# The state-space part and the output mixing in one block, with the chunk sums formed turned

## The chip, the cores and the metric

The kernel runs on one core of one Trainium2 chip. The metric is the device time of one execution in microseconds (us), lower is better; times shown for a version are medians of several runs. PE is TensorE's matmul, PEld its weight load, DVE is VectorE, ACT ScalarE, POOL GpSimd, SP SyncE, which here only issues DMAs.

## What is computed

The whole model has a first block (convolution and RWKV mixing, then a channel mix) and two hybrid layers. Only the second half of a hybrid layer is touched:

```python
# 1024 tokens, width 1024; 16 state-space heads of 64, 2 groups, state 128, chunks of 128 tokens
attn = sliding_window_attention(q, k, v, sinks) * silu(z_attn)
y = ssd_chunked(xs, dt, a, bm, cm)
#   y_diag = cb * exp_segsum(a_cs) @ (x*dt)      within a chunk
#   y_off  = cc @ prev_state * exp(a_cs)         from the state before the chunk
#   state  = prev_state * exp(a_cs[-1]) + b^T @ (x * dt * decay_to_end)
y = y + xs * d_skip
g = y * silu(z_ssm)
ssm = g * rsqrt(mean(g*g over a group of 512) + eps) * ssm_norm_w
out = concat([attn, ssm]) @ w_out                # 2048 x 1024
x = layer_norm(alpha * x + out)
```

## The kernel before, in words

Everything is float32. Big products are made as three products of parts (high by high, high by low, low by high) in the matmul type fp32r: `high` on ScalarE casts, `low` on VectorE subtracts. Each engine has its own instruction list, written out by hand; they meet by semaphores alone, so the order in each list is fixed, and an engine that waits holds up all that stands behind in its list. The DMAs from SP have SP's order too.

For each layer `second_layer` (L2837) runs an attention block, then `state_space_and_attention_out` (L2178), then `state_out_and_norm` (L2648).

**L2178** works through eight chunks c of 128 tokens and fills TensorE's list with pieces of attention @ w_out. A unit u is one token tile by 512 of the 1024 output columns, eight pieces of three products of 512 columns (`fill`, L2305, one PSUM bank OUT); the add of a unit to the residual frees the bank (`add`, L2544). TensorE's work for a chunk: `b_and_cb` (L2319, L2321) turns B and forms C·B; `from_state` (L2336) multiplies the state; `to_state` (L2344) forms the chunk's state; `within` makes the skip products (L2356) and 16 head products (L2361: the masked decays E[:, h], 128x128, stationary; x·dt of the head, 64 columns, moving; each product is two passes, as all in plain float32); `x_turned` (L2329) turns the next chunk's x; `y_turned` (L2370) turns y with eight transposes, so that the channel is on the partition; `square_sums` (L2380) and `spread` (L2391) give the inverse root mean square to all partitions. VectorE masks the decays (`weigh`, L2562), scales x (`inputs`, L2569, L2570), scales what came from the state by exp of the running sum, with a column per head broadcast over the head (L2612, EI), adds (L2631), multiplies by the gate (L2577), inverts (L2581) and normalises (L2586, one instruction over 1024 columns). ScalarE makes the decays: 16 floors (L2485) and an exponential (L2490) a chunk, with a table load where a root (L2502) came before. POOL splits weights (L2442, L2444) and lets the state decay (L2452).

SP's list in the loop: wait for `yd(c)` (the end of the head products), then decay rows for chunk c+3 (L2228, 1 MB), inputs for c+2 (L2232), at c = 4 six weight pieces that each wait for the split two before, then the store of y for c-1 (L2249, waits for the normalisation) and the gates for c+1 (L2235, two buffers). y goes to DRAM.

**L2648** multiplies y (read back, scaled by `norm_w_2` on the way into its parts, L2738, L2762) by the other 1024 rows of w_out: weights outer, eight PSUM banks, with the last five weight pieces kept for the end, so that the layer norm of a token tile (L2768 to L2783) runs beside the products (L2693) of the next.

## Time and profile before

| | us |
|---|---|
| median of 3 runs | 3448.87 |
| lowest, highest | 3447.88, 3450.91 |
| the profiled execution | 3451.71 |
| its span in the trace | 3449.8 |
| PE busy | 3145.1 (91%) |
| DVE busy | 1482.6 (43%) |
| ACT busy | 1061.8 (31%) |
| POOL busy | 996.3 (29%) |
| mean granted TensorE clock | 0.953 |

Busy is the union of an engine's instructions. PE's shows how dense its list is, and not that it works at its peak: a matmul's row includes its pipeline (a product of 512 columns is shown with some 390 ns and starts 230 ns behind the one before). The clock is a share of 2.4 GHz; TensorE runs at 1.2 or 2.4. A view by stretches of time (us from the span's start) shows where an engine stands; the waits show behind what.

### The profile page before, as it was taken

The numbers are of one execution on the slowest core, as the hardware profiler recorded it, in microseconds if no ns is written. First come the engines' busy times: TensorE is split into PE (matmuls) and PEld (weight loads), VectorE is DVE, ScalarE is ACT, GpSimd is POOL, SyncE is SP. The second block draws the span as 40 slices with busy tenths as digits, with TensorE's granted clock in tenths as the row PEclk, the third lists the DMA queues.
The fourth block names the chain that finished last, engine by engine and source line by source line (L and its number), as shares of the span: only waits on it lengthen the run. The fifth ranks groups of instructions, "written<-read, shape, count | busy, mean of one in ns | idle before, by whom it ended". The sixth has DMA issues, their size and how long they took to land. (4 is left out here: it accounts for less than half of the span.)

```text
span 3449.8 us, 49680 instructions
## 1 busy us (share of the span) xinstructions
PE 3145.1 (91%) x21066; PEld 2491.3 (72%) x21066; DVE 1482.6 (43%) x2152; ACT 1061.8 (31%) x1832; POOL 996.3 (29%) x658
## 2 busy tenths in 40 slices
PE   5998799785999998998999998788999999978888
PEld 3886498674888887887777776566777777756667
DVE  3999644434222224342243342554412433425544
ACT  3012333323222222222243443541213444444411
POOL 2443022103333323322333332221323333321212
PEclk8999799897999999999999999899999999988999
DMA  5113300122111111123111222653331112226432
GB/s 199 49 49 116 105 4 4 44 100 93 47 48 49 49 36 52 60 95 100 50 61 62 74 86 91 217 147 104 114 86 50 62 62 74 92 104 204 144 113 102
DMA packets 296327, 292.82 MB, mean 85 GB/s; under 512 B 10784, under 2 KB 252832, under 8 KB 291648
## 3 DMA queue, kind: packets, MB, share of 16 engines
q1 hardware_dynamic: 252320, 235.28, 21.5%
q10 hardware_dynamic: 43808, 54.66, 4.6%
q8 instruction: 152, 2.49, 0.3%
q14 instruction: 47, 0.39, 0.0%
HBM read 233.16 MB, written 54.66 MB: 83 GB/s over the span
## 5 line engine op out<-in xcount | busy, mean ns | idle before, releaser
L1880 PE MATMUL PS<-x_high_sb,w_high_sb 128*128 128x512 f32 x1312 | 530.1, 404 | 0.0
L1880 PE MATMUL PS<-x_high_sb,w_low_sb 128*128 128x512 f32 x1312 | 518.2, 395 | 0.0
L1880 PE MATMUL PS<-x_low_sb,w_high_sb 128*128 128x512 f32 x1312 | 517.4, 394 | 0.0
L1880 PEld LDWEIGHTS PS<-x_high_sb,w_high_sb 128*128 128x128 f32 x1312 | 246.9, 188 | 76.1 <-issue 23.9
L1880 PEld LDWEIGHTS PS<-x_high_sb,w_low_sb 128*128 128x128 f32 x1312 | 246.8, 188 | 57.8
L360 PE MATMUL PS<-h_high_sb,up_high_sb 128*128 128x512 f32 x704 | 274.7, 390 | 14.1 <-POOL up_low_sb L1445 14.1
L1880 PEld LDWEIGHTS PS<-x_low_sb,w_high_sb 128*128 128x128 f32 x1312 | 247.3, 188 | 52.4
L360 PE MATMUL PS<-h_low_sb,up_high_sb 128*128 128x512 f32 x704 | 274.6, 390 | 0.0
L360 PE MATMUL PS<-h_high_sb,up_low_sb 128*128 128x512 f32 x704 | 274.4, 390 | 0.0
L1495 DVE SCALAR_TENSOR_TENSOR z_sb<-PS,cols_sb,z_sb 128x1023 f32<-128x1023 f32 x88 | 112.8, 1282 | 348.5 <-ACT z_sb L1476 342.1
L2118 DVE CUSTOM_DVE_ANT_0 scores_sb<-PS,alibi_sb,sinks_sb 128x256 f32<-128x256 f32 (+1 forms) x256 | 104.4, 465 | 342.5 <-PE PS L1898 342.5
L1980 POOL CAST w_high_sb<-w_raw_sb 128x1024 fp32r<-128x1024 f32 x80 | 83.0, 1037 | 522.1 <-PE PS L1880 514.0
L496 DVE SCALAR_TENSOR_TENSOR mix_sb<-rkq_sb,cols_sb,mix_sb 128x1024 f32<-128x1024 f32 x120 | 197.7, 1648 | 3.8
L1982 POOL TENSOR_TENSOR w_low_sb<-w_raw_sb,w_high_sb 128x1024 fp32r<-128x1024 f32 x80 | 192.1, 2401 | 6.4
L1992 POOL TENSOR_TENSOR scores_sb<-scores_sb,inverse_sums_sb 128x1024 f32<-128x1024 f32 (+1 forms) x64 | 114.4, 1787 | 202.4 <-DVE inverse_sums_sb L2136 202.4
L2305 PE MATMUL PS<-w_high_sb,attn_high_sb 128*128 128x512 f32 x256 | 126.0, 492 | 41.9 <-POOL w_low_sb L2444 29.1
L360 PEld LDWEIGHTS PS<-h_high_sb,up_high_sb 128*128 128x128 f32 x704 | 132.6, 188 | 42.0 <-POOL up_low_sb L1445 14.4
L2070 ACT COPY probs_turned_sb<-PS 128x512 f32<-128x512 f32 x56 | 32.8, 587 | 420.8 <-PE PS L1913 420.8
L360 PE MATMUL PS<-h_high_sb,w_high_sb 128*128 128x512 f32 x368 | 145.5, 395 | 11.7 <-DVE values_sb L337 7.9
L360 PEld LDWEIGHTS PS<-h_low_sb,up_high_sb 128*128 128x128 f32 x704 | 132.6, 188 | 27.5
L360 PEld LDWEIGHTS PS<-h_high_sb,up_low_sb 128*128 128x128 f32 x704 | 132.6, 188 | 27.5
L1564 PE MATMUL PS<-down_high_sb,mid_high_sb 128*128 128x512 f32 x352 | 138.4, 393 | 12.3 <-POOL down_low_sb L1556 12.0
(414 smaller groups left out, 6316.6 us busy)
## 6 DMA issues: line engine op xcount, KB each, us to landing
w_raw_sb<-w_in SPq DMA_DIRECT2D x102, 512.0 KB, 3.8
up_raw_sb<-w_up SPq DMA_DIRECT2D x44, 512.0 KB, 3.8
ada_slots_sb<-ada_w SPq DMA_DIRECT2D x16, 1024.0 KB, 5.9
attn_raw_sb<-attn ACTq DMA_DIRECT2D x32, 512.0 KB, 4.7
decays_sb<-running_sums SPq DMA_DIRECT2D x16, 1024.0 KB, 5.2
w_raw_sb<-w_out SPq DMA_DIRECT2D x64, 256.0 KB, 3.5
xbc<-staged_sb ACTq DMA_DIRECT2D x24, 512.0 KB, 2.6
xbc_sb<-xbc SPq DMA_DIRECT2D x16, 768.0 KB, 6.9
```

What stands on the lines that cost most here:

```text
L360: last = pe.matmul(m.PS[:, bank, :], a[:, k], b[:, k, half * NH:(half + 1) * NH], start=k == 0 and a is WH and b is HH, stop=k == KT - 1 a ...
L496: ins = v.scalar_tensor_tensor(out=out, in0=u, scalar=w, in1=out, op0=ALU.mult, op1=ALU.add)
L1495: ins = v.scalar_tensor_tensor(out=z, in0=bank2(m, n)[:, 0:T - tap], scalar=col("ffn_w", i * 6 + (j + c * FT) * 3 + 2 - tap), in1=z, op0=A ...
L1564: last = pe.matmul(PS[:, k, :], a[:, i % SLOTS, k * P:(k + 1) * P], b[:, i % SLOTS], start=q == 0 and a is MH and b is WH, stop=q == FT - ...
L1880: last = pe.matmul(PS[:, bank, :], a[:, n % 2, k], b[:, k, cols], start=k == 0 and a is WH and b is HH, stop=k == KT - 1 and a is WL)
L1980: nc.gpsimd.tensor_copy(WH[:, n % 2], raw).then_inc(s.wchain, 1)
L1982: nc.gpsimd.tensor_tensor(WL[:, n % 2], raw, WH[:, n % 2], ALU.subtract).then_inc(s.split, 1)
L1992: nc.gpsimd.tensor_tensor(p, p, RD[:, u % 2].unsqueeze(2).to_broadcast([P, G4, 2 * P - lo(nb)]), ALU.mult).then_inc(s.probs, 1)
L2070: nc.scalar.copy(PT[:, u % 2, 0], PS[:, 2 * (u % 2), :]).then_inc(s.moved0, 1)
L2118: ins = v.tensor_tensor_reduce(SC[:, u % 2, i, lo(nb):2 * P], PS[:, 2 * (u % 2) + i % 2, at + lo(nb):at + 2 * P], BIAS[:, g % 2, i, lo(nb) ...
L2305: last = pe.matmul(PS[:, OUT, :], a[:, u % 2, q], b[:, q], start=q == 0 and a is AH and b is WH, stop=q == KT - 1 and a is AL)
```

## The change

`state_space_and_mix` takes the place of both functions. There are 32 units now: attention by the first and second column half of w_out (units 0 to 15), then y by both halves (16 to 31). Two are done before the loop over chunks, two in each iteration, the rest behind it, from unit 18 on in four banks in turn. Its weights come in 32 pieces with ten slots; the first eight are loaded at once and split by ScalarE and VectorE, the others by POOL at three places. y is stored to and read back from DRAM chunk by chunk, and the layer norm runs in the same block.

The sums of a chunk are formed turned, the channel on the partition: x·dt (64 columns) is stationary, alternately in the lower and upper 64 columns of the array, and the decays move (128 columns). The state is stationary in `from_state`, in eight tiles. So `y_turned` is gone. The factor exp of the running sum is now needed along the tokens and not by a column per head: `rate_rows` loads it from DRAM (ER, one buffer, two DMAs of 256 KB a chunk), `rates` forms the exponential on ScalarE. The gate z has one buffer in place of two. The normalisation also multiplies by `norm_w_2`, in eight instructions. Squares are written over Y. The diff, cut to its core:

```diff
-def state_space_and_attention_out(m, d_skip, xbc_d, gate_d, rows_d, attn_d, y_d, src, w, DT, A, NA, EI, DE, CD):
+def state_space_and_mix(m, layer, d_skip, xbc_d, gate_d, rows_d, attn_d, y_d, src, w, ln_g, ln_b, dst, ahead,
+                        DT, A, NA, EI, DE, CD):
...
-    UNITS = 2 * TT
+    SLOTS, WS = 3, 10
+    UNITS, FREE = 4 * TT, 2 * TT + 2
...
-        ZS = alloc(m, ctx, "z_gate", [P, 2, KT, P])
+        ZS = alloc(m, ctx, "z_gate", [P, KT, P])
+        ER = alloc(m, ctx, "rates", [P, KT, P])
+        WH = alloc(m, ctx, "w_high", [P, WS, NH], F32R)
+        WL = alloc(m, ctx, "w_low", [P, WS, NH], F32R)
...
+        bank = lambda u: OUT if u < FREE else (u - FREE) % 4
+        before = lambda u: u if u < FREE else u - 3
+        def slot_empty(eng, i):
+            j, q = (i - WS) // KT, (i - WS) % KT
+            if q == KT - 1:
+                eng.wait_ge(s.prod, TT * (j + 1))
+            else:
+                eng.wait_ge(s.piece, (KT - 1) * j + q + 1)
+        part = lambda h: slice(h % 2 * HD, (h % 2 + 1) * HD)
+        turned = lambda h: PS[part(h), 2 + h // 8, h % 8 // 2 * P:(h % 8 // 2 + 1) * P]
...
         def _(sp):
+            def rate_rows(c):
+                if c >= 2:
+                    sp.wait_ge(s.yo_out, c - 1)
+                pairs = rows_d[c * SH:(c + 1) * SH].rearrange("(q a) t -> a q t", a=2)
+                for a in range(2):
+                    sp.dma_start(ER[part(a)], pairs[a:a + 1].to_broadcast([HD, KT, P])).then_inc(s.er_in, 16)
             def gates(c):
-                sp.dma_start(ZS[:, c % 2], chunk(gate_d[:, :, cols(c)])).then_inc(z_in[c % 2], 16)
+                if c:
+                    sp.wait_ge(s.gate, c)
+                sp.dma_start(ZS[:], chunk(gate_d[:, :, cols(c)])).then_inc(s.z_in, 16)
...
             inputs(0)
+            sp.dma_start(skip[:], d_skip.to_broadcast([P, SH])).then_inc(s.skip_in, 16)
+            first_weights(0)
+            first_weights(1)
+            residual(0)
             rows(0)
+            residual(1)
             rows(1)
             inputs(1)
+            rate_rows(1)
             weights(8)
             weights(9)
+            rows(2)
+            gates(0)
+            residual(2)
             for c in range(TT):
                 sp.wait_ge(s.yd, c + 1)
                 if c + 3 < TT:
                     rows(c + 3)
                 if c + 2 < TT:
                     sp.wait_ge(s.x, c + 1)
                     inputs(c + 2)
-                if c == 4:
-                    for i in range(10, 2 * KT):
-                        weights(i)
+                if c and c + 1 < TT:
+                    rate_rows(c + 1)
+                for i in {1: range(10, 12), 2: range(12, 20), 6: range(20, 27)}.get(c, ()):
+                    weights(i)
                 if c:
                     store(c - 1)
-                    if c + 1 < TT:
-                        gates(c + 1)
+                    gates(c)
...
         def _(pe):
             def from_state(c):
-                for g in range(SG):
-                    last = pe.matmul(PS[:, 2 + g, :], XB[:, c % 2, KT + SG + g], S[:, c % 2, g * GW:(g + 1) * GW],
-                                     start=True, stop=True)
+                for q in range(KT):
+                    last = pe.matmul(PS[:, 2 + q // 4, q % 4 * P:(q % 4 + 1) * P], S[:, c % 2, q * P:(q + 1) * P],
+                                     XB[:, c % 2, KT + SG + q // (KT // SG)], start=True, stop=True)
             def within(c):
-                    pe.matmul(PS[:, 2 + q // 4, (q % 4) * P:(q % 4 + 1) * P], XB[:, c % 2, q], SKIP[:, q],
+                    pe.matmul(PS[:, 2 + q // 4, (q % 4) * P:(q % 4 + 1) * P], SKIP[:, q], XB[:, c % 2, q],
...
-                    last = pe.matmul(PS[:, 2 + h // 8, (h % 8) * HD:(h % 8 + 1) * HD], E[:, c % SLOTS, h],
-                                     XDT[:, h * HD:(h + 1) * HD], start=False, stop=True, skip_group_check=True)
+                    last = pe.matmul(turned(h), XDT[:, h * HD:(h + 1) * HD], E[:, c % SLOTS, h], start=False, stop=True,
+                                     skip_group_check=True)
-            def y_turned(c):
...
+            fill(2 * KT)
             for c in range(TT):
                 if c + 1 < TT:
                     b_and_cb(c + 1)
+                fill(1)
                 if c:
                     from_state(c)
+                fill(2)
                 if c < TT - 1:
                     to_state(c)
                 fill(2)
                 if c:
+                    square_sums(c - 1)
+                fill(2)
                 within(c)
+                fill(1)
                 if c + 1 < TT:
                     x_turned(c + 1)
+                fill(2)
                 if c:
                     spread(c - 1)
+                fill(6)
+            fill(KT)
             square_sums(TT - 1)
+            fill(KT)
             spread(TT - 1)
+            fill(len(pieces))
...
         def _(pool):
+            pool.wait_ge(s.wfirst, KT)
+            for i in range(KT, WS):
+                split(i)
+            for c in range(1, 4):
+                grow(c)
+            for i in range(WS, WS + KT):
+                split(i)
+            for c in range(4, TT - 1):
+                grow(c)
+            for i in range(WS + KT, 4 * KT):
+                split(i)
...
         def _(act):
+            def rates(c):
+                act.wait_ge(s.er_in, 32 * c)
+                nc.scalar.activation(ER[:], ER[:], ACT.Exp, scale=-1.0).then_inc(s.rates, 1)
...
+            high(0)
+            for i in range(KT):
+                first(i)
             act.wait_ge(s.kept, 1)
             floors(0)
             exps(0)
-            high(0)
             high(1)
             floors(1)
             exps(1)
+            high(2)
             for c in range(TT):
+                a = 2 * c + 2
                 if c + 1 < TT:
                     move(c + 1)
                 if c:
+                    square(c - 1)
+                high(a + 1)
+                if c:
+                    root(c - 1)
                 if c + 2 < TT:
                     floors(c + 2)
+                if c + 1 < TT:
+                    rates(c + 1)
                 if c + 2 < TT:
                     exps(c + 2)
+                high(a + 2)
...
         def _(dve):
             def gate(c):
-                dve.wait_ge(s.g, c + 1)
-                dve.wait_ge(z_in[c % 2], 16 * (c // 2 + 1))
+                dve.wait_ge(s.y, c + 1)
+                dve.wait_ge(s.z_in, 16 * (c + 1))
             def normalise(c):
                 dve.wait_ge(s.spread, 2 * c + 2)
-                h = YT[:, c % 2].rearrange("p (g k) n -> p g k n", g=SG)
-                v.tensor_tensor(h, h, PS[:, G_RS, 0:P].unsqueeze(2).to_broadcast([P, SG, KT // SG, P]), ALU.mult
-                                ).then_inc(s.normed, 1)
+                for q in range(KT):
+                    h = YT[:, c % 2, q]
+                    ins = v.scalar_tensor_tensor(out=h, in0=h, scalar=m.col("norm_w_2", layer * KT + q),
+                                                 in1=PS[:, 6 + q // (KT // SG), 0:P], op0=ALU.mult, op1=ALU.mult)
+                ins.then_inc(s.normed, 1)
...
             for c in range(TT):
+                a = 2 * c + 2
+                add(a - 1)
+                low(a + 1)
                 if c:
                     dve.wait_ge(s.yo, c)
+                    dve.wait_ge(s.rates, c)
-                    v.tensor_tensor(by_head(y), heads(YO_YD), wide(EI, c), ALU.mult).then_inc(s.yo_out, 1)
+                    v.tensor_tensor(by_tile(y), tiles(YO_YD), ER[:], ALU.mult).then_inc(s.yo_out, 1)
...
                 if c + 1 < TT:
                     inputs(c + 1)
+                add(a)
+                low(a + 2)
                 if c:
                     invert(c - 1)
                     normalise(c - 1)
+                gate(c)
...
-def state_out_and_norm(m, layer, w, ln_g, ln_b, y_d, dst, ahead):
```

The rest: `load` of a y unit waits for its store; `add` of the y units also sums rows; `centre`, `norm` and `finish` are the layer norm as before; the last five weight pieces are loaded into room freed by Y and the state.

## Rows read from the trace of the kernel before

**Rows 1.** Stretches of layer 1: PE, PEld, DVE, ACT, POOL busy, PEclk, DMA share, GB/s.

```profile
2141.30:2190.40 49.10, 22.20 (x104) 18.00 (x104) 17.76 (x18) 23.88 (x56) 19.39 (x17) 0.69 0.94 319
...
2266.00:2291.40 25.40, 24.75 (x168) 19.20 (x166) 16.65 (x16) 13.19 (x25) 7.40 (x5) 1.00 0.53 156
2291.40:2318.10 26.70, 17.39 (x85) 11.12 (x85) 8.55 (x9) 5.68 (x14) 11.22 (x12) 0.74 0.58 180
...
2395.50:2408.10 12.60, 0.01 (x1) 0.04 (x1) 2.84 (x3) 1.15 (x1) 3.11 (x3) 0.63 0.51 169
2408.10:2498.10 90.00, 89.65 (x384) 73.39 (x384) 35.44 (x62) 18.83 (x28) 34.04 (x30) 0.98 0.36 123
```

**Rows 2.** Waits of PE, 2141 to 2400: total us, times, longest.

```profile
PE PS L2319 <- DMA xbc_sb<-xbc: 26.8, 3, 11.3
PE PS L2305 <- POOL w_low_sb L2444: 14.8, 6, 6.5
```

**Rows 3.** Timeline of PE, 2255 to 2300: start, us, instruction.

```profile
2256.86 1.04 PE L2370 MATMUL PS<-consts_sb,y_sb 128*128 128x128 f32 x8
...
2259.11 1.95 PE L2356 MATMUL PS<-skip_diagonal_sb,xbc_sb 128*128 128x128 f32 x16
2260.89 3.68 PE L2361 MATMUL PS<-x_dt_sb,decays_sb 128*128 128x64 f32 x32
...
2265.16 1.04 PE L2329 MATMUL PS<-consts_sb,xbc_sb 128*128 128x128 f32 x8
...
2268.83 0.65 PE L2380 MATMUL PS<-gated_squares_sb,consts_sb 128*32 128x64 f32 x32
...
2271.68 0.94 PE L2391 MATMUL PS<-inverse_rms_sb,consts_sb 32*128 32x64 f32 x8
...
2275.86 1.88 PE L2336 MATMUL PS<-state_sb,xbc_sb 128*128 128x512 f32 x4
...
2278.96 1.88 PE L2344 MATMUL PS<-x_dt_decayed_sb,b_and_cb_sb 128*128 128x512 f32 x4
```

**Rows 4.** Timeline of PE in the attention block, stationary 128x64.

```profile
3058.00 1.09 PE L1923 MATMUL PS<-probs_turned_sb,v_sb 128*64 128x256 f32 x8
```

**Rows 5.** Timeline of PE, 2150 to 2200, chunk 0.

```profile
2181.58 3.02 PE L2356 MATMUL PS<-skip_diagonal_sb,xbc_sb 128*128 128x128 f32 x16
```

**Rows 6.** DMA issues, 2190 to 2395: count, KB each, median us to landing.

```profile
attn_raw_sb<-attn ACTq DMA_DIRECT2D x13, 512.0 KB, 4.0
...
xbc_sb<-xbc SPq DMA_DIRECT2D x5, 768.0 KB, 6.9
...
z_gate_sb<-gate SPq DMA_DIRECT2D x6, 512.0 KB, 6.1
```

**Rows 7.** Timeline of SP, 2283 to 2320, iteration 4.

```profile
2290.20 0.43 SPq L2232 DMA_DIRECT2D xbc_sb<-xbc  x1
2290.68 16.27 SPq L2245 DMA_DIRECT2D w_raw_sb<-w_out  x6
2310.93 0.38 SPq L2249 DMA_DIRECT2D state_out<-y_turned_sb  x1
```

**Rows 8.** Timeline of ACT, 2273 to 2300.

```profile
2275.39 1.05 ACT L2472 CAST attn_high_sb<-attn_raw_sb 128x1024 fp32r<-128x1024 f32 x1
2276.34 4.78 ACT L2485 ACTIVATE decays_sb<-decays_sb,dta_sb 128x128 f32<-128x128 f32 x16
...
2286.78 1.91 ACT L2490 ACTIVATE decays_sb<-decays_sb 128x2048 f32<-128x2048 f32 x1
```

**Rows 9.** Timelines of DVE, 2140 to 2182 and 2255 to 2274.

```profile
2158.13 3.67 DVE L2598 TENSOR_TENSOR skip_diagonal_sb<-consts_sb,skip_rows_sb 64x1024 f32<-64x1024 f32 x2
...
2265.75 0.68 DVE L2544 SCALAR_TENSOR_TENSOR HT_sb<-HT_sb,PS 128x512 f32<-128x512 f32 x1
2266.50 1.22 DVE L2536 TENSOR_TENSOR attn_low_sb<-attn_raw_sb,attn_high_sb 128x1024 fp32r<-128x1024 f32 x1
...
2269.90 0.55 DVE L2581 RECIPROCAL inverse_rms_sb<-inverse_rms_sb 128x64 f32<-128x64 f32 x1
```

More of the change, by code:

```diff
@@ L2623, in _ @@
                     masked(c + 1)
-                if c:
-                    gate(c - 1)
                 if c + 1 < TT:
@@ L2797, in first_block @@
+            for u in range(FREE + 2, UNITS):
+                if u + 1 < UNITS:
+                    low(u + 1)
+                add(u)
+                k = u - (UNITS - TT)
+                if k >= 0:
+                    centre(k)
+                    if k:
+                        finish(k - 1)
+            finish(TT - 1)
 def first_block(m, gate, x_mid, dst, ahead):
```

396 lines of the change are left out of this document (152 added, 244 removed).

## The prediction, made before the change was run

> **What bounds the kernel now.** I first read the stretches of one second-block layer; the second layer's look the same. The state-space block runs from 2141.3 to 2395.5 us, 12.6 us follow in which TensorE does nothing, and the second block of the layer needs 90.0 us for its 384 products, with TensorE busy all the time [rows 1]: 0.234 us a product, and 0.70 us for a piece of three. From 2141.3 to the last product at 2498.1 a layer takes 356.8 us, and this is the length that I compare. In the undisturbed iteration from 2266.0 to 2291.4 TensorE is busy 24.75 of 25.4 us at full clock: that stage is TensorE's own. The waits say where it isn't: 26.8 us for state-space inputs (mostly the start, and the iteration in which SP stood at the weights) and 14.8 us for split weights [rows 2]. So the change gains what it takes off TensorE, as long as no engine's order makes TensorE wait for something new.
>
> **What it takes off TensorE.** The eight turns of y, 1.04 us as a row and 0.8 us from start to start [rows 3], go: 6.5 us a layer. The head products change from 32 passes of 64 columns with a full-width stationary tile (3.68 us for 32, 0.11 us each) to 32 passes of 128 columns, whose 64-wide stationary tiles go alternately to the two column halves. The trace has no such product here, but the attention's last product has this shape with 256 columns: 8 passes end in 1.09 us, less some 0.38 us of pipeline 0.10 us a pass [rows 4], where 512 columns take 0.43 us from start to start (1.88 us for four, less the pipeline) [rows 3] and 256 one after another would take 0.21. The halves run side by side. At 128 columns I take 0.056 us a pass, 1.8 us for 32, a gain of 1.8 us a chunk and 14 us a layer. The bounds are 0.05 and 0.11 us a pass (no overlap). The skip products and the product from the state keep their columns. With the 12.6 us gap this is some 33 us a layer, if nothing waits.
>
> The Trainium skill (TensorE: Matmul & The Clock Gate, on what overlaps and what doesn't) says that a weight load overlaps a running product only where the row group differs; here all rows are used by both halves. By it each pass would show its load too, and the head products would take no less than before. The rows of the attention speak against it.
>
> **What it adds: three loads in the path of a chunk.** I follow iteration c from the moment when its first piece may start (0), that is when VectorE has added unit 2c+1.
>
> 1. To the end of the head products. Pieces 1+2+2+2 (4.9 us), from the state and to the state 1.7 each, square sums 0.6, skip 1.8, heads 1.8 [rows 3]: 12.5 us. After an idle time like the one worked out in step 5 TensorE starts at 1.2 GHz: the skip products took 3.02 us in place of 1.95 after a wait for split weights [rows 3, 5]; the stretches with long waits have a mean granted clock of 0.69 and 0.74 [rows 1]. I add 2 us (bounds 0 and 3): 14.5.
> 2. Rate rows. ER has one buffer, and SP issues its next load behind its wait for the end of the head products, behind the decay rows (1 MB) and the inputs (0.79 MB). The inputs land 6.9 us after their issue, which is 0.4 us after that end [rows 6, 7]. Two more loads of 256 KB at 319 GB/s [rows 1] are 1.6 us: landed at 9.1 us after the heads (bounds 7 and 12), 23.6. ScalarE has the root behind the square sums (9.9), then 16 floors of 4.8 us together [rows 8] and a table load of a good 1 us: it is at the wait by 16 and stands some 8 us.
> 3. Behind that wait on ScalarE are queued: rates 1.1 (between half of exps and the cast), exps 1.9, the cast high(2c+4) 1.05 [rows 8]. VectorE's low(2c+4) (1.2) waits for the cast, and the reciprocal (0.55) is behind low [rows 9]. TensorE's spread waits for the reciprocal. 23.6+5.9=29.5. TensorE itself would have come to the spread after piece, x turned, two pieces: 3.1 us after the heads, at 17.6. It loses 12 us. In these also lies a smaller new stall: the add of unit 2c+2 now stands behind both input products on VectorE, 3.2 us.
> 4. Spread 0.9, then the normalisation, now eight instructions of 128 columns: the trace has none; between 0.15 (an eighth of 1.22) and 0.42 us each, I take 0.23 as a quarter of the 0.68 for 512 columns [rows 9] with some start cost: 1.8. At 32.2.
> 5. The gate z also has one buffer, and its load is issued by SP behind store(c-1), which waits for this very normalisation. VectorE's next instruction, gate(c), waits for that load. z's load takes 6.1 us from issue now [rows 6], behind a store and beside the attention load; I take 6.0 from the normalisation's end (bounds 5.3 and 8.5). In the kernel before nothing waits for z, which has two buffers and is loaded well ahead. Then the gate 1.2, and only then add(2c+3) 0.7: 32.2+6.0+1.9=40.1. TensorE has six pieces and the turned B for this time, 5 us; it stands another 4 to 5 us.
>
> So the iteration goes from 25.2 to **40.1 us**. Chunk 5 has no decay rows in front (38). In chunk 2 SP also stands at eight weight loads, the last of them behind the split of the eighth piece, before it comes to the store and the gate. The pieces must first be used by unit 7, whose third piece stands behind the late spread; the split pace is that of the present iteration 4, six loads in 16.3 us [rows 7]. The split ends at 45, z lands at 51.5, the add at 53. In chunk 6 seven loads do the same: 44.4 us.
>
> **Head and tail of a layer.** The block starts with 2 MB of first weights, residual, decay rows, all at about 319 GB/s [rows 1]. To the end of chunk 0's decay rows that is 5.5 MB with the attention's two loads, 17 us from 2147: they land at 2164, and high(1) is behind floors(0) and exps(0) on ScalarE: 2173. VectorE then has low(1), the two skip products (3.67 us, rows 9) and add(0) before unit 1 may start: 2178.6, some slow products, ready for the loop at 2185.8. Chunk 0 has neither rates nor gate waits, 22.7 us to the next first piece: 67 us from the start. After iteration 6, the last: heads at 12.9, unit 17 at 21.7, unit 18 at 27.2 beside gate(7) (26.3, its z late as before), unit 19 from 29.8 to 35.3, spread 36.2, twelve units of 5.45 us with 2 us for late splits: 103.5. What comes behind the last product (add, centre, square, root, two passes: 6.9 us before) stays within 1 us, since two rows' work also lay there.
>
> Sum a layer: 67+3×40.1+38+53+44.4+103.5=426.2, against 356.8: +69.4, for two layers **+139 us**. Rate and weight DMAs of the rest and POOL's other work are on no path: POOL is at the state's growth only 1.9 us in 25. The profiled execution took 3451.7 us (span 3449.8), the median of the runs 3448.9: 3590.5 on the first, **3588** on the second.
>
> **Rivals.** (A) *Rates don't hold* (3509): if the rate rows land by the time ScalarE has done its floors, chunks 1 to 4 lose 7.7 us less, chunk 5 5.6, chunk 6 3: 39.4 a layer. For it: only 0.5 MB is added. Against: the place in SP's order is plain, and the inputs alone take 7.3 us from the same moment. 8%. (B) *Neither late load is felt* (3379), the faster side: its place is SP's two waits; it decides where both land within the work that TensorE still has. Then an iteration is bound by ScalarE's order, heads 12.5, floors, rates, exps, cast, low, reciprocal to 20.1, spread and six pieces to 26; 67+6×26+98=321, 36 less than now a layer. It needs a z landing in under 1.5 us after issue; no load in the trace does [rows 6]. 7%, most of it for a misreading of mine in the order. (C) *The halves don't overlap* (3616): 1.8 us a chunk comes back in chunks 1 to 7 and 0, 14 a layer. By the skill's rule above this is what would come. 6%. (D) *The waits are dearer* (3650 and up): loads of 512-byte pieces at half the rate, slow clock also behind the spread: 3 us on each of ten of the loop's iterations and more at the weights. 10%, partly in the range. (E) The change does as it says, yet PE has so much less to do that it is neither: within 0.2%, 1%.
>
> The Trainium skill (DMA: Bandwidth & Descriptors, the two cost components) gives a load 2.0 us and its bytes over 436 GB/s, an estimate of 3.2 us for z. With it the iteration would be 2.8 us shorter and the time about 3555; the attention load of the same size, with less before it, shows 4.0 us [rows 6].
>
> **Numbers.** The forecast has 68%. Its own bounds: landing of rates −2/+3, z −0.7/+2.5, normalisation −0.6/+1.5, clock −2/+1, seldom all together, −4/+6 us on 12 iterations and 5 us on each head and tail: 3535 to 3660. With (A) and (C) and part of (D): 3500 to 3670. A measurement of this kernel tells 0.2% (7 us) from no change. Faster 0.07 (B), same 0.01, slower 0.92.
>
> **What will show it.** In the new profile ScalarE should wait about 8 us before the exponential of the rates, for a DMA from the running sums, five times a layer; TensorE before the spread products some 12 us, put down to the reciprocal; VectorE before the gate product some 6 us, put down to the load of z, seven times; both longer in chunks 2 and 6. The head products should stand as 32 in about 2.2 us with their pipeline, and the gap before the state's half of the output should be gone. The iteration should be near 40 us. If TensorE's wait before the spread is under 4 us, step 3 is wrong; if the gate waits under 2 us, step 5 is; if both hold and the time is below 3500, the head or tail is.

## The result, and the profile after

The changed kernel takes 3625.57 us (median of 4 runs, 3620.71 to 3627.39) beside 3448.39 us for the kernel before on the same chip (4 runs, 3447.88 to 3450.91): a ratio of 1.051, interval 1.0492 to 1.0528, 177.2 us slower. The forecast was 3588 us with a range of 3500 to 3670: direction, mechanism and range hold, and the point is 37.6 us low.

The profiled execution took 3625.99 us (span 3624.2, granted clock 0.929; before 0.953). The engines' totals on the first lines of the page:

```profile
span 3624.2 us, 50028 instructions
...
PE 3149.7 (87%) x21106; PEld 2498.5 (69%) x21106; DVE 1537.0 (42%) x2298; ACT 1104.0 (30%) x1886; POOL 949.1 (26%) x626
```

TensorE was busy 3145.1 us before. It should have had less to do; it has as much, since it now works longer at a low clock, and it stands for some 170 us more. From the end of the last attention product to the end of the last product of the block's output (the length that the prediction compares), layer 1 takes 451.1 us (356.8 before) and layer 2 444.2 (357.7): +94.3 and +86.5, together 180.8. The code outside was some microseconds quicker in this execution (layer 1 began 4.4 us earlier), so 174.3 us remain between the two profiled executions.

The windows of layer 1 after the change, cut at the first piece of each iteration; the columns are those of [rows 1]. The first is iteration 1, then 2 to 6; the last row is the head, from 2141.3 as before (the layer itself now begins at 2136.8):

```profile
2206.60:2247.30 40.70, 25.82 (x171) 20.13 (x171) 17.52 (x22) 14.68 (x27) 1.90 (x1) 0.79 0.44 123
2247.30:2303.90 56.60, 27.06 (x170) 21.34 (x171) 17.61 (x22) 13.61 (x26) 16.79 (x17) 0.71 0.41 116
2303.90:2346.70 42.80, 26.68 (x170) 21.38 (x171) 17.60 (x22) 13.76 (x26) 1.91 (x1) 0.82 0.39 105
2346.70:2389.60 42.90, 27.07 (x170) 21.18 (x171) 17.61 (x22) 13.69 (x26) 1.90 (x1) 0.76 0.39 104
2389.60:2429.30 39.70, 28.37 (x170) 22.25 (x171) 17.60 (x22) 13.72 (x26) 1.91 (x1) 0.74 0.34 86
2429.30:2474.60 45.30, 23.19 (x164) 18.02 (x164) 17.02 (x22) 6.81 (x8) 15.90 (x16) 0.83 0.35 99
...
2141.30:2206.60 65.30, 39.69 (x182) 31.57 (x182) 31.50 (x37) 32.09 (x69) 6.58 (x5) 0.76 0.88 270
```

The undisturbed iteration of before was 25.4 us with TensorE busy 24.75 and the clock at 1.00 [rows 1]. Now it is 40 to 43 us, TensorE is busy 26 to 28 of them, and the mean clock is 0.74 to 0.82: it works longer on the same pieces, because after its stops the products stand 0.43 us apart for some microseconds in place of 0.23.

The waits of layer 1, from 2141 to 2560 (total us, times, longest), those that the forecast named and those on TensorE:

```profile
DVE y_turned_sb L2693 <- issue: 60.4, 6, 20.0
...
ACT rates_sb L2554 <- DMA rates_sb<-running_sums: 54.3, 6, 10.3
...
PE PS L2440 <- DVE inverse_rms_sb L2697: 46.4, 7, 9.9
PE PS L2360 <- DVE HT_sb L2639: 45.7, 14, 11.4
...
PE PS L2360 <- issue: 32.5, 2, 16.6
```

The two loads are there as two standing engines (the first two rows: the gate's wait ends with z's load, which SP had only just issued, and the profile puts that down to "issue"). TensorE feels the first as the wait for the reciprocal. The second is in its waits for VectorE's add (L2639), 11.8 us of them (four, before the first pieces of iterations 2, 4, 5 and 6), and in the 32.5 us of "issue" before those of iterations 3 and 7. The rest of the 45.7 us is not z: 11.4 us are the head's, and 21.9 are seven stops of 3.13 us, one an iteration, for the add that stands behind both input products on VectorE (step 3 of the forecast). They are a loss of their own, which moving the two loads leaves where it is. One iteration shows the chain. ScalarE, iteration 4 (start, us, instruction, idle before it):

```profile
2356.39 4.77 ACT L2561 ACTIVATE decays_sb<-decays_sb,dta_sb 128x128 f32<-128x128 f32 x16
2361.18 1.28 ACT L2554 ACT_TABLE_LOAD   x1
2372.77 1.06 ACT L2554 ACTIVATE rates_sb<-rates_sb 128x1024 f32<-128x1024 f32 x1 [10.30 <-DMA rates_sb<-running_sums]
...
2373.73 1.89 ACT L2566 ACTIVATE decays_sb<-decays_sb 128x2048 f32<-128x2048 f32 x1
2375.53 1.03 ACT L2530 CAST attn_high_sb<-attn_raw_sb 128x1024 fp32r<-128x1024 f32 x1
```

VectorE, the same iteration:

```profile
2376.59 1.23 DVE L2627 TENSOR_TENSOR attn_low_sb<-attn_raw_sb,attn_high_sb 128x1024 fp32r<-128x1024 f32 x1 [10.44 <-ACT attn_high_sb L2530]
2377.73 0.55 DVE L2697 RECIPROCAL inverse_rms_sb<-inverse_rms_sb 128x64 f32<-128x64 f32 x1
2379.83 2.15 DVE L2703 SCALAR_TENSOR_TENSOR y_turned_sb<-y_turned_sb,cols_sb,PS 128x128 f32<-128x128 f32 x8 [1.55 <-PE PS L2440]
2387.65 1.23 DVE L2693 TENSOR_TENSOR y_turned_sb<-y_and_state_sb,z_gate_sb 128x1024 f32<-128x1024 f32 x1 [5.67 <-issue]
2388.80 0.68 DVE L2639 SCALAR_TENSOR_TENSOR HT_sb<-HT_sb,PS 128x512 f32<-128x512 f32 x1
```

TensorE, the same iteration. Its row of heads stands where the forecast put it. Of the three waits behind it the first is the add behind the input products, the other two are the two loads at second hand:

```profile
2359.43 1.97 PE L2416 MATMUL PS<-decays_sb,x_dt_sb 128*64 128x128 f32 x32
...
2366.30 0.47 PE L2360 MATMUL PS<-w_high_sb,attn_high_sb 128*128 128x512 f32 x1 [3.13 <-DVE HT_sb L2639]
...
2378.33 1.45 PE L2440 MATMUL PS<-inverse_rms_sb,consts_sb 32*128 32x64 f32 x8 [9.87 <-DVE inverse_rms_sb L2697]
...
2389.62 0.47 PE L2360 MATMUL PS<-w_high_sb,attn_high_sb 128*128 128x512 f32 x1 [2.77 <-DVE HT_sb L2639]
```

And SP's queue, which releases both:

```profile
2361.43 0.33 SPq L2256 DMA_DIRECT2D decays_sb<-running_sums  x1
2361.81 0.43 SPq L2267 DMA_DIRECT2D xbc_sb<-xbc  x1
2362.29 4.49 SPq L2264 DMA_DIRECT2D rates_sb<-running_sums  x2
2382.01 0.36 SPq L2294 DMA_DIRECT2D state_out<-y_turned_sb  x1
2382.42 0.58 SPq L2272 DMA_DIRECT2D z_gate_sb<-gate  x1
```

SP is released at 2361.4, when the heads end, issues decay rows and inputs, and only then the rates. It is released again at 2382.0, when the normalisation ends, stores and only then issues z.

### The profile page after: what moved, and what is told of

Its sections match the earlier page's. It is cut to its first block and busy times, and to the rows that moved or that the text cites. A ratio compares the mean times of both kernels' runs of the same rounds, so it can differ in the third digit from the quotient of the medians.

```text
span 3624.2 us, 50028 instructions
## 1 busy us (share of the span) xinstructions
PE 3149.7 (87%) x21106; PEld 2498.5 (69%) x21106; DVE 1537.0 (42%) x2298; ACT 1104.0 (30%) x1886; POOL 949.1 (26%) x626
## 3 DMA queue, kind: packets, MB, share of 16 engines
q1 hardware_dynamic: 266944, 242.63, 21.8%
## 5 line engine op out<-in xcount | busy, mean ns | idle before, releaser
L2360 PE MATMUL PS<-w_high_sb,attn_high_sb 128*128 128x512 f32 x512 | 240.7, 470 | 173.6 <-DVE HT_sb L2639 89.7
L1880 PEld LDWEIGHTS PS<-x_high_sb,w_high_sb 128*128 128x128 f32 x1312 | 247.0, 188 | 76.1 <-issue 23.8
L2360 PEld LDWEIGHTS PS<-w_high_sb,attn_high_sb 128*128 128x128 f32 x512 | 109.7, 214 | 215.2 <-issue 176.7
L2360 PE MATMUL PS<-w_low_sb,attn_high_sb 128*128 128x512 f32 x512 | 221.4, 432 | 0.0
L2360 PE MATMUL PS<-w_high_sb,attn_low_sb 128*128 128x512 f32 x512 | 220.8, 431 | 0.0
L360 PE MATMUL PS<-h_high_sb,w_high_sb 128*128 128x512 f32 x368 | 145.5, 395 | 12.2 <-DVE values_sb L337 7.9
```

The costliest lines, as they stand in the source:

```text
L360: last = pe.matmul(m.PS[:, bank, :], a[:, k], b[:, k, half * NH:(half + 1) * NH], start=k == 0 and a is WH and b is HH, stop=k == KT - 1 a ...
L1880: last = pe.matmul(PS[:, bank, :], a[:, n % 2, k], b[:, k, cols], start=k == 0 and a is WH and b is HH, stop=k == KT - 1 and a is WL)
L2360: last = pe.matmul(PS[:, bank(u), :], a[:, u % 2, q], b[:, i % WS], start=q == 0 and a is AH and b is WH, stop=q == KT - 1 and a is AL)
```

## The experiments

Two questions stand behind the time. Is it the place of the two loads in SP's order, as the forecast says, or something else about the new block (a costlier turned form, contention of more bytes, halves that don't overlap)? And what are the 37.6 us that the forecast missed? All edits are against the changed kernel unless said otherwise. The ratios are to the kernel before, which took 3449.84, 3449.39 and 3447.41 us in the three batches. Iterations are those of layer 1, from first piece to first piece.

**1. The rate rows earlier.** They are issued at the top of SP's iteration, ahead of its wait for the end of the head products. The buffer is free by then: the exponential before has been used.

```
             for c in range(TT):
+                if c and c + 1 < TT:
+                    rate_rows(c + 1)
                 sp.wait_ge(s.yd, c + 1)
...
-                if c and c + 1 < TT:
-                    rate_rows(c + 1)
```

> The changed kernel with one thing moved: SP issues the rate rows of chunk c+1 ahead of its wait for the end of the head products (they then wait only for the product that used the last ones). Same transfers, same bytes. Theory (places in the lists): ScalarE's wait before the rates (10 us an iteration) goes, TensorE's wait before the spread with it; about 10 us in iterations 1, 3, 4, about 8 in 2 and 5, 1 to 2 in 6 (bound by the weight loads there), 48 us a layer: some 3530 us. Rival (contention: the added 16 MB of loads slow the others): the transfers are the same, so within 10 us of 3625.

Measured: 3541.96 us, ratio 1.0272 (1.0251 to 1.0292), 83.6 us less than the changed kernel and 12 us above what I had expected. The iterations from 1 on are 32.2, 46.5, 33.1, 32.2 and 35.1 us. ScalarE's wait for the rates is gone from the list of waits, the spread products stand directly behind the pieces, and VectorE's wait for z stays (the waits of this run, 2141 to 2480):

```profile
DVE y_turned_sb L2693 <- issue: 61.6, 6, 20.9
```

Step 2 and step 3 of the forecast are one cause, and it is the place of this load.

**2. The gate's load earlier.** gates(c) is taken from behind store(c-1) to the top of the iteration.

```
             for c in range(TT):
+                if c:
+                    gates(c)
                 sp.wait_ge(s.yd, c + 1)
...
                     store(c - 1)
-                    gates(c)
```

> The changed kernel with the load of the gates for chunk c moved to the top of SP's iteration, so that it waits for gate(c-1) alone and not for the store of y behind the normalisation and the weight loads. Theory: VectorE's wait before the gate product goes (5.7 us in a plain iteration, 20 in iteration 2, 17 in iteration 6), but TensorE has work for all but 2.7 us of the plain ones; with 16 and 15 us in iterations 2 and 6 and 3 in the tail that is 45 us a layer: some 3535 us. The wait before the spread stays (10 us). Rival (contention): within 10 us of 3625.

Measured: 3525.76 us, ratio 1.0225 (1.0204 to 1.0245), 99.8 us less, 9 us more than expected. The iterations are 37.5, 37.4, 43.8, 38.3 and 34.5. VectorE's gate follows the normalisation at once, and TensorE's waits for the add fall to 34.4 us, nearly all of it the head's and the seven of 3.13 us; the wait behind the rates stays as it was (the waits of this run, 2141 to 2480):

```profile
ACT rates_sb L2555 <- DMA rates_sb<-running_sums: 59.6, 6, 15.2
PE PS L2441 <- DVE inverse_rms_sb L2698: 48.3, 7, 14.0
```

This is step 5. In iteration 2 it also takes away what the eight weight loads had cost by standing before z: 56.6 us became 37.4.

**3. Both.** If the two loads are the whole loss, this kernel keeps what the change takes off TensorE. The edit is that of 1 and 2 together.

> Both loads moved as in the two runs before. Theory: a plain iteration takes 27 to 28 us (from 42.8), iterations 2 and 6 about the same, since neither the spread nor the gate waits for SP any more; 103 us a layer: some 3415 us, faster than the kernel before the change (3448). What then stays in a plain iteration is the add that stands behind both input products on VectorE (3.2 us of TensorE) and the reciprocal behind the cast of the next piece (1 to 2 us). Rival (contention, or a lower clock that stays): 3600 or more. Rival (the two moves only uncover each other's wait): the better of the two runs before, some 3530.

Measured: 3447.33 us, ratio 0.9992 (0.998 to 1.0003). That is the time of before and not below it: 32 us above what I had expected. The iterations are 29.8, 27.1, 39.0, 25.9 and 28.6. Of SP's queue in iterations 2 and 3:

```profile
2260.98 20.15 SPq L2290 DMA_DIRECT2D w_raw_sb<-w_out  x8
2281.17 0.43 SPq L2294 DMA_DIRECT2D state_out<-y_turned_sb  x1
2281.65 0.58 SPq L2272 DMA_DIRECT2D z_gate_sb<-gate  x1
2282.27 2.32 SPq L2264 DMA_DIRECT2D rates_sb<-running_sums  x2
```

and ScalarE in the same stretch:

```profile
2291.91 1.06 ACT L2555 ACTIVATE rates_sb<-rates_sb 128x1024 f32<-128x1024 f32 x1 [11.39 <-DMA rates_sb<-running_sums]
```

SP stands at the eight weights for 20 us, each waiting for POOL to split an earlier one, and whatever is next in its order is late. Moving the rates and z up in one iteration only moved them behind the weights of the iteration before. So a third cause is left, SP's stand at the weights, which the forecast had only as a lengthening of z's wait; and the other iterations are still above the 24 us that the work needs. Experiments 5 and 7 take up the weights, experiment 6 the other iterations.

**4. The head products of one column half, then of the other.** This tests whether alternating the column halves is what makes them quick (rival C). The eight heads of one half (16 passes) come first, then the eight of the other.

```
-                for h in range(SH):
-                    if h % 8 == 0:
-                        pe.wait_ge(s.masked, 2 * c + h // 8 + 1)
+                pe.wait_ge(s.masked, 2 * c + 2)
+                for h in [*range(0, SH, 2), *range(1, SH, 2)]:
```

> The changed kernel with the 16 head products in another order: first the eight of the lower column half, then the eight of the upper, so that no two neighbours use different halves. Theory (the halves run side by side only when they alternate): 32 passes take 3.6 us in place of 1.97, on the path in eight chunks of both layers: 26 us more, some 3652 us. Rival (64 columns are cheap for another reason, as a shorter weight load): 2.0 us as before and within 5 us of 3625.

Measured: 3649.22 us, ratio 1.0583 (1.0562 to 1.0604), 23.7 us more where I had expected 26. The head products of one iteration on TensorE's timeline:

```profile
2365.05 3.33 PE L2415 MATMUL PS<-decays_sb,x_dt_sb 128*64 128x128 f32 x32
```

3.33 us in place of 1.97, 1.36 us a chunk, 21.8 us for sixteen chunks. Less the 0.38 us of pipeline that the prediction takes off, a pass takes 0.050 us alternately and 0.092 apart; the skip products, also of 128 columns but with a stationary tile of full width, take 0.098 (1.95 us for 16 [rows 3]). So apart a pass costs what any pass of 128 columns costs here, and alternately two run in the time of one. The edit also makes TensorE wait for both masks before its first product; that wait isn't in the row. I ran the same edit once more on the fastest kernel below (experiment 9).

**5. The weight loads last.** Store and gate load come ahead of the weight loads in SP's iteration; the waits for rates and z stay as in the changed kernel.

```
-                for i in {1: range(10, 12), 2: range(12, 20), 6: range(20, 27)}.get(c, ()):
-                    weights(i)
                 if c:
                     store(c - 1)
                     gates(c)
+                for i in {1: range(10, 12), 2: range(12, 20), 6: range(20, 27)}.get(c, ()):
+                    weights(i)
```

> The changed kernel with one thing moved: in SP's iteration the store of y and the load of the gates stand ahead of the weight loads. Theory: iteration 2 takes what a plain one takes (43 us from 56.6) and iteration 6 about 40 (from 45.3); some of it comes back in iterations 3 and 7, whose loads then stand behind the weight loads: 15 us a layer, some 3595 us. Rival (the weights themselves are what iterations 2 and 6 wait for): within 5 us of 3625.

Measured: 3574.86 us, ratio 1.0362 (1.0341 to 1.0383), 50.7 us less, 20 more than expected. Iteration 2 went from 56.6 to 42.0 us, iterations 1, 3, 4 and 5 moved by 0.3 to 3.0 us either way, and iteration 6 from 45.3 to 34.9, where I had expected 40: TensorE's stop before the first piece of iteration 7, 15.9 us behind the seven weights and z, is 3.8 us. In two layers that is half of the 20 us; the rest of the layer behind it is only 1.5 us shorter. Layer 1 is 427.2 us.

**6. The order on VectorE.** On the kernel of experiment 3: the add before the input products' instructions, and the reciprocal before low, so that neither the next unit nor the spread stands behind work that nobody needs yet.

```
+                add(a)
                 if c + 1 < TT:
                     inputs(c + 1)
-                add(a)
-                low(a + 2)
                 if c:
                     invert(c - 1)
+                low(a + 2)
+                if c:
                     normalise(c - 1)
```

> Both loads first, and VectorE's list in another order: add of unit 2c+2 ahead of the two input products, the reciprocal ahead of low(2c+4). Theory: in the plain iterations TensorE no longer stands 3 us for the add; from 27.5 us to about 24; iteration 3, in which SP is still at the weight loads and the rates come late (39 us), stays. Five or six iterations less 3 us in two layers: some 3415 us. Rival (the add and the cast are covered by other work by now): within 7 us of 3447.

Measured: 3398.34 us, ratio 0.985 (0.9831 to 0.987), 49.0 us less than experiment 3, 17 more than expected. The iterations are 25.5, 23.9, 35.9, 28.1 and 23.9: where no load is late, an iteration is now shorter than the 25.4 us of before. The 3.2 us stall of step 3 was real: in experiment 3 TensorE stands 3.13 us for this add in each of iterations 0 to 6, here 0.24 to 0.83, which in two layers is some 39 of the 49 us. For the reciprocal it stands 10.5 us in iteration 3 of experiment 3 and 1.04 here, but there it now waits 9.0 us for the next inputs, which SP issues behind the weights, and 2.5 for the add.

**7. The weight loads issued by POOL.** On the kernel of experiment 6: POOL, which splits a weight and so frees its buffer, issues the next load itself, on semaphores of their own. SP's loop then has no weights in it.

```
             for i in range(KT, 4 * KT):
...
                 nc.gpsimd.tensor_tensor(WL[:, i % WS], piece, WH[:, i % WS], ALU.subtract).then_inc(s.wsplit, 1)
+                if i + 2 < 4 * KT - len(LATE):
+                    pool.wait_ge(s.wsplit, i - KT + 1)
+                    pool.dma_start(RAW[:, i % 2], piece_of(i + 2)).then_inc(own_in[i % 2], 16)
```

> As the order run, and the weight loads are issued by POOL behind its own splits, not by SP. Theory: nothing of SP's list waits for a split now, so iteration 3 falls from 39 to about 24 us and 6 is plain: 15 us a layer more, some 3385 us. Rival (iteration 3 is long because its weights are late): within 7 us of the order run.

Measured: 3379.98 us, ratio 0.9797 (0.9777 to 0.9817), 18.4 us less, 5 more than expected. The iterations are 25.5, 23.8, 29.0, 25.4 and 23.9, layer 1 328.5 us. Iteration 3 went from 35.9 to 29.0: that was SP's stand at the weights. Most of the rest, down to the 24 us that I had expected, is what the rival named: the weights themselves are late there. TensorE stands 2.80 us for POOL's split in it, here as in experiment 8, and runs some products slowly behind the stop:

```profile
2268.40 0.79 PE L2359 MATMUL PS<-w_high_sb,attn_high_sb 128*128 128x512 f32 x1 [2.80 <-POOL w_low_sb L2493]
```

**8. Head and tail.** On the kernel of experiment 7: at the head ScalarE's cast high(1), VectorE's low(1) and add(0) come ahead of the first chunk's decays, inputs and skip products; at the tail ScalarE makes the casts of POOL's last five late weights, so that POOL only subtracts.

```
+            high(1)
             act.wait_ge(s.kept, 1)
             floors(0)
             exps(0)
-            high(1)
+            high(2)
...
-            inputs(0)
             low(1)
+            inputs(0)
+            add(0)
             dve.wait_ge(s.skip_in, 16)
...
-                nc.gpsimd.tensor_copy(WH[:, i % WS], piece).then_inc(s.wchain, 1)
+                if i < LAST:
+                    nc.gpsimd.tensor_copy(WH[:, i % WS], piece).then_inc(s.wchain, 1)
```

> As the run with POOL's loads, and at the start unit 1's cast, its low part and the add of unit 0 come ahead of the floors, exponentials and skip products of chunk 0; at the end ScalarE casts the last five weight pieces, so that POOL only subtracts. Theory: unit 1 starts some 8 us earlier, of which some 8 a layer stay; the unit whose weights come late (9.7 us in place of 5.5) loses its wait, 3 to 4 us a layer: 22 us less than the run before, some 3363 us. Rival (the start is bound by its 9 MB of loads): only the 7 us of the tail.

Measured: 3366.70 us (3362.35 to 3370.34), ratio 0.9762 (0.9746 to 0.9778), 4 us above what I had expected. It is the fastest kernel of the study, 83 us below the kernel before in the same batch. The first piece of iteration 0 comes 38.8 us after the layer's start in place of 46.5, the stretch from the first piece of iteration 6 to the end takes 127.5 us in place of 133.1, and the layer 315.9 us. The two edits weren't run apart. In it the head products stand as they did:

```profile
2263.96 1.97 PE L2416 MATMUL PS<-decays_sb,x_dt_sb 128*64 128x128 f32 x32
```

**9. The halves apart, where TensorE is what counts.** The edit of experiment 4 on the kernel of experiment 8.

> The fastest version so far (3367 us) with the head products of one column half behind those of the other, as in the halves-apart run. Here TensorE is the bound of a plain iteration (23.8 us). Theory: 32 passes take 3.6 us again, 1.7 us in each of 16 chunks: 27 us, some 3393 us. Rival (part of it is covered by waits that are left): 10 us or less.

Measured: 3381.75 us, ratio 0.9807 (0.9779 to 0.9836), 15 us more and not 27. The products take the same 3.33 us as before, 1.36 us more a chunk and 21.8 for sixteen. The 15 us are not simply that with a part hidden: the undisturbed iterations grew from 23.8 to 26.8, by 3.0 us. Iteration 2 of both kernels (the columns are those of [rows 1]), experiment 8 first:

```profile
2224.60:2248.40 23.80, 22.29 (x171) 17.62 (x171) 17.37 (x22) 13.56 (x26) 7.51 (x8) 1.00 0.69 194
```

```profile
2229.60:2256.40 26.80, 25.30 (x173) 20.13 (x172) 17.64 (x22) 13.78 (x26) 8.36 (x9) 0.94 0.68 187
```

The other 1.6 us are clock: behind the spread some eight products of 512 columns stand 0.43 us apart there, at a mean granted clock of 0.94, where experiment 8 has 1.00 and 0.23 throughout. The longest stop before them is 1.0 us in both kernels, so what lowers the clock in the one isn't seen here. Against this, TensorE's wait for POOL's split weights in layer 1 fell from 5.0 to 0.7 us and iteration 3 from 28.9 to 26.7. The 15 us are what is left of the three.

**10. The rates behind the heads, but ahead of the other rows.** This sizes the term of step 2. In the changed kernel the rate rows stay behind SP's wait for the heads, but go ahead of the decay rows and the inputs.

```
                 sp.wait_ge(s.yd, c + 1)
+                if c and c + 1 < TT:
+                    rate_rows(c + 1)
                 if c + 3 < TT:
                     rows(c + 3)
...
-                if c and c + 1 < TT:
-                    rate_rows(c + 1)
```

> The changed kernel with the rate rows still behind SP's wait for the head products, but ahead of the decay rows and the inputs. Theory: they land some 5 us after the heads in place of 11.3; ScalarE's wait falls from 10 to some 4 us; 6 us in iterations 1 to 5 of both layers: some 3565 us. Rival (what holds them is the number of descriptors of 512 bytes, not what stands ahead): they land as late as before, within 10 us of 3625.

Measured: 3581.91 us, ratio 1.0388 (1.0357 to 1.0418), 43.7 us less; I had expected 17 more than that. The iterations are 35.7, 51.0, 37.9, 36.9 and 35.1, 4.6 to 6.0 us less each. SP, and then ScalarE, in iteration 4 of this run:

```profile
2350.57 1.26 SPq L2264 DMA_DIRECT2D rates_sb<-running_sums  x2
2351.88 0.62 SPq L2256 DMA_DIRECT2D decays_sb<-running_sums  x1
```

```profile
2355.98 1.06 ACT L2554 ACTIVATE rates_sb<-rates_sb 128x1024 f32<-128x1024 f32 x1 [4.35 <-DMA rates_sb<-running_sums]
```

With nothing ahead of them the two loads are issued in 1.26 us and land 5.4 us after the heads; behind the decay rows and the inputs SP needs 4.49 us for the two issues and they land 11.3 us after them (2361.4 to 2372.7). So their place behind the other rows costs 6 us an iteration, the wait for the heads itself the rest. The rival, that their many pieces of 512 bytes make them late whatever stands ahead, is refuted.

The experiments as a table, against the changed kernel (3625.57 us):

| experiment | us | less than changed |
|---|---|---|
| rates ahead of SP's wait | 3541.96 | 83.6 |
| rates first behind that wait | 3581.91 | 43.7 |
| z ahead of SP's wait | 3525.76 | 99.8 |
| weights behind z | 3574.86 | 50.7 |
| both loads ahead | 3447.33 | 178.2 |
| and VectorE's order | 3398.34 | 227.2 |
| and POOL's own loads | 3379.98 | 245.6 |
| and head and tail | 3366.70 | 258.9 |

The two loads alone and together nearly add up (83.6 + 99.8 = 183.4 against 178.2), as two causes that stand one behind the other in an iteration do.

## Why the prediction was right, and what was mis-sized

**The mechanism.** All signs that it named but one are in the trace. ScalarE waits before the rates, down to the DMA from the running sums, 54.3 us in layer 1, six times, 9 us each, where I had said five times 8; TensorE before the spread, put down to the reciprocal, 9.9 us in iteration 4, which with the 3.13 at the add before it makes 13 for my 12; VectorE before the gate, seven times, 5.7 us in a plain iteration. The gate's wait is longer in iterations 2 and 6, 20.0 and 17.5 us; the one before the spread, which I had also called longer there, is not: 9.8 us in 2, and 3.0 in 6. Experiments 1 and 2 remove one each and leave the other, experiment 3 both. So the cause is shown: the two loads sit in single buffers behind waits of SP that have nothing to do with them.

**The gain was there.** The head products take 1.97 us for 3.68 before [rows 3], 1.7 us a chunk where I had 1.8, and the turns and the gap of 12.6 us are gone (10.5 us now stand at the layer's end before the next block, 11.1 before). Experiment 7 shows the gain once the waits are gone: layer 1 takes 328.5 us against 356.8, layer 2 321.3 against 357.7, 28 and 36 us beside the 33 that I gave to it. With a better head and tail layer 1 takes 315.9. Its orders of VectorE and of the weight loads weren't tried on the kernel before, so how much of this they would give there isn't known.

**Step by step, iteration 4, times from its first piece at 2346.7:**

| step | predicted | measured |
|---|---|---|
| 1 heads end | 14.5 | 14.7 |
| 2 rates landed | 23.6 | 26.0 |
| 3 spread | 29.5 | 31.6 |
| 4 normalised | 32.2 | 35.3 |
| 5 gate starts | 38.2 | 41.0 |
| next first piece | 40.1 | 42.9 |

Step 1 holds, 2 us of lower clock included (other iterations vary). *The term that failed is the landing in step 2:* I put the rates behind 1.8 MB at the block's rate of bytes, 9.1 us after the heads (its own terms, 7.3 and 1.6, give 8.9), and measured 11.3. Two things are off in it. I had taken SP's issues as free; here the second issue of rate rows is itself held, and the pair takes 4.49 us on SP, where it takes 1.26 with nothing ahead (experiment 10). And I had taken 319 GB/s for the rate of bytes, where the stretch from the heads' end to the landing has 208 (last column):

```profile
2361.40:2372.80 11.40, 3.93 (x17) 2.59 (x17) 4.17 (x4) 1.09 (x2) 0.00 (x0) 0.75 0.81 208
```

The runs don't separate the two. The bound that I had given (7 to 12 us) holds it. The second term is step 4: the spread takes 1.45 us at the lower clock where I had 0.9, and the eight instructions of the normalisation 2.15 us, 0.27 each, where I took 0.23. Steps 3 and 5 are right in length: 5.6 us from landed rates to the spread for 5.9, 5.7 to the gate for 6.0. TensorE's own stop for the gate is 2.8 us where I had 4 to 5, since its six pieces behind the spread begin at the lower level.

**Which iterations.** Forecast 40.1, 53, 40.1, 40.1, 38 and 44.4; measured 40.6, 56.6, 42.8, 42.9, 39.7 and 45.3 (2206.7 to 2474.6): 267.9 us for 255.7, +12.2. Iteration 2's 3.6 are in the rows: z, behind the eight weights, is issued at 2296.2, 48.9 us after the iteration's start, where I had it landed at 51.5. SP's queue there:

```profile
2269.88 25.82 SPq L2290 DMA_DIRECT2D w_raw_sb<-w_out  x8
2295.74 0.43 SPq L2294 DMA_DIRECT2D state_out<-y_turned_sb  x1
2296.22 0.58 SPq L2272 DMA_DIRECT2D z_gate_sb<-gate  x1
```

**Head and tail.** The head is 69.9 us for 67: unit 1 starts where I put it (at 2173.97, 37.1 us after the layer's start for 37.3), but after an idle time of 11.45 us the next pieces run 0.43 us a product for over 5 us before they come to 0.23, and the loop's first piece comes 9.2 us after it for 7.2. I had counted "some slow products". The tail is 113.3 us for 103.5. Up to the spread of the last chunk it holds (36.8 for 36.2), the rest takes 9 us more than twelve units of 5.45 us and 2 us. Two stops in it were not in my sum. The store and reload of the last chunk's y hold unit 23, and the last weights, which POOL can begin to split only when that unit's first products are through, and then in some 2 us each, hold unit 24. TensorE's four stops in the two units, of which two are shown, are 4.7 us together, and behind the first and the last some products are again 0.43 us apart. TensorE there:

```profile
2531.39 0.80 PE L2360 MATMUL PS<-w_high_sb,attn_high_sb 128*128 128x512 f32 x1 [2.55 <-DVE attn_low_sb L2627]
...
2542.84 0.50 PE L2360 MATMUL PS<-w_high_sb,attn_high_sb 128*128 128x512 f32 x1 [0.92 <-POOL w_low_sb L2491]
```

and POOL, which stood 64.93 us before the first of these splits:

```profile
2533.18 1.48 POOL L2489 CAST w_high_sb<-w_raw_sb 128x512 fp32r<-128x512 f32 x1 [64.93 <-PE PS L2360]
```

In experiment 8, where ScalarE makes these casts, the tail is 5.6 us shorter than in experiment 7. The three parts, 2.9 + 12.2 + 9.8, are the 24.9 us by which layer 1 exceeds the forecast; layer 2 exceeds it by 18.0. Of the 42.9 us together 0.9 was there before the change (layer 2 took 357.7 us and not 356.8), and 6.5 were made up by quicker code elsewhere. That leaves the 35.5 us between the forecast for the profiled execution (3590.5) and its time (3625.99); between the medians it is 37.6.

**The rivals.** (A), the rates don't hold: refuted by 54.3 us of wait and by experiment 1. (B), neither is felt: refuted for this order, yet it is what the kernel becomes when the order is mended: (B) gave 321 us a layer and iterations of 26, experiment 8 has 315.9 and 23.8. (C), the halves don't overlap: refuted, 1.97 us for 32 alternating passes. By the rule of the Trainium skill (TensorE: Matmul & The Clock Gate, The mechanism, on what overlaps and what doesn't) that a weight load overlaps running products only where the row group differs, every pass would have shown its load in either order, and the two orders should have cost the same. This case doesn't bear it out: with all rows in use by both, experiment 4 shows 1.97 against 3.33 us. (D), dearer waits, is the part of the error that was left: 3 us in about ten iterations was its condition, and in layer 1 0.5 to 3.6 came. The figure of the Trainium skill for z (DMA: Bandwidth & Descriptors, Anatomy of one DMA, the two cost components: 2.0 us and bytes over 436 GB/s, an estimate of 3.2 us) doesn't agree with this trace, where 512 KB of z land 5.2 us after the issue behind a store (the median of seven in the DMA issues, 2190 to 2500, and 8.3 us for the rate rows from theirs):

```profile
z_gate_sb<-gate SPq DMA_DIRECT2D x7, 512.0 KB, 5.2
rates_sb<-running_sums SPq DMA_DIRECT2D x12, 256.0 KB, 8.3
```

**What stays open.** Layer 2 is 7 us shorter than layer 1 in the changed kernel, 1.6 us in the head, 4.4 in iterations 1 to 5 (54.2 us for 56.6 in iteration 2) and 0.9 behind; why isn't known. The two moves of experiment 6 weren't run apart, so the division of its 49 us is read from the waits and not tested. Whether it is the lower rate of bytes or SP's held issue that makes the rates land late isn't known either.

## What to carry to other kernels

When a load is added to a kernel in which one engine issues all loads in order, what counts is the wait ahead of it in that list: two loads of 0.5 MB a chunk cost 178 us here behind waits for other work, and that came back when they were issued one wait earlier. A single-buffered operand should be issued as soon as its own buffer is free, and a load that must wait for a slow consumer (the weights for POOL) belongs to the consumer's own queue. And a saving of TensorE shows in the time only when the engines around it are ordered by who waits for them: with nothing but the order of loads and of VectorE's instructions altered, the same change went from 5.1% slower to 1.5% faster.

## What the runs showed of the hardware that I had not expected

- *An issue of a load can itself take microseconds on SP.* Two loads of 256 KB are issued in 1.26 us with nothing ahead of them and in 4.49 us behind 1.8 MB; at the layer's head, behind several megabytes issued in the 10 us before, SP's row for the two spans 15.76 us. Whether the bytes or the number of pieces ahead hold it, the runs don't tell:

```profile
2151.43 15.76 SPq L2264 DMA_DIRECT2D rates_sb<-running_sums  x2
```

- *Column halves of one row group run side by side only when they alternate pass by pass:* 0.06 us a pass against 0.10, pipeline included, the same products and the same data. The 0.10 is what a pass of 128 columns with a full-width tile also takes.
- *A stop costs more than its length.* After waits of 8 to 11 us TensorE ran at its lower level (0.43 us for a 512-column product in place of 0.23) for 5 to 6 us. The fall needn't come with the stop: behind the 3.13 us at 2366.3 the first products are 0.23 us apart, and 0.8 us later they are 0.43 apart. The mean granted clock of a plain iteration, with one wait of 6 to 10 us and two of 2 to 4 us, was 0.74 to 0.82, and TensorE's busy time 1 to 4 us more than in the undisturbed one of before, although it had less to do.
